# Decays and two delta-rule units in the last HGRN head, and memory pieces in pairs beside the early units

## The reference, cut to what matters

```python
# first layer
h = rmsnorm(x, attn_norm[i]);  mem_n = rmsnorm(mem, mem_norm[i])       # mem: 256 x 1024
cols = split_cols(h @ dsa_w_in[a], DSA_COLS)                           # indexer, latent, queries
k, v = jnp.split(mem_n @ w_kv_mem, 2, axis=-1)                         # memory attention, later
# hybrid layer: 8 HGRN heads, then 8 pairs of delta-rule heads
(hq, hf, hi, hg, gq, gk, gv, ga, gb, gz, gate_h, gate_g) = jnp.split(u @ w_in, offsets, axis=-1)
o_h = rmsnorm_2(hgrn2_chunked(...), hgrn_out_norm) * silu(hg)
qkv = silu(causal_short_conv(concatenate([gq, gk, gv]), conv_w))
beta = sigmoid(gb)
g = -exp(a_log) * softplus(ga + dt_bias)                               # the decays
gam = cumsum(g, axis=-1)                                               # per chunk
```

## Time and profile before

| | |
|---|---|
| median of 3 runs | 3383.93 us (3383.03 to 3387.18) |
| profiled execution | 3391.74 us, its span 3389.9 us |
| TensorE busy | 3216.2 us, 95% |
| VectorE / ScalarE / GpSimd busy | 1580.0 / 1419.1 / 1585.7 us |
| mean granted clock of TensorE | 0.97 of full |
| HBM read | 241.51 MB, 72 GB/s over the span |

### The profile page before, as it was taken

How to read it: one execution, slowest core, us unless ns; L and a number is a source line. 1 busy time by engine, 2 the same in 40 slices (tenths; PEclk the granted TensorE clock), 3 DMA queues, 4 the chain that set the end, 5 groups by cost and what they waited for, 6 DMA issues and landing times.

```text
span 3389.9 us, 44791 instructions
## 1 busy us (share of the span) xinstructions
PE 3216.2 (95%) x16754; PEld 2650.5 (78%) x16754; DVE 1580.0 (47%) x2189; ACT 1419.1 (42%) x2479; POOL 1585.7 (47%) x1361
## 2 busy tenths in 40 slices
PE   5889999999999999999989886999999999999998
PEld 4567888877788887888867775888888888888887
DVE  4783443146533322443077774555565652233321
ACT  3355333226743333333255544544554432243332
POOL 4345444665554456445542222444444434564454
PEclk8989999999999999999999987999999999999999
DMA  4212333341033333333322210111111123333332
GB/s 120 56 38 63 96 96 95 98 126 45 2 93 99 94 97 89 99 93 95 97 64 55 56 44 25 38 38 38 38 38 38 38 56 95 98 93 99 93 94 81
DMA packets 471621, 246.86 MB, mean 73 GB/s; under 512 B 13883, under 2 KB 468774, under 8 KB 471334
## 3 DMA queue, kind: packets, MB, share of 16 engines
q1 hardware_dynamic: 470144, 241.33, 25.2%
q10 hardware_dynamic: 1318, 3.35, 0.3%
HBM read 241.51 MB, written 2.10 MB: 72 GB/s over the span
## 4 chain that ended last, share of the span: by engine, by line
PE 86%; DVE 7%; ACT 3%; issue 3%; POOL 1%; DMA 0%; POOLq 0%; ACTq 0%; DVEq 0%
PE ps L465 19%; PE ps L466 19%; PE ps L467 19%; PE ps L2450 2%; PE ps L2346 2%; PE ps L2347 2%; PE ps L2348 2%; PE ps L2432 2%; PE ps L1645 2%; PE ps L1669 2%; PE ps L1655 2%; PE ps L1865 1%; PE ps L1938 1%; PE ps L1866 1%; PE ps L1867 1%
## 5 line engine op out<-in xcount | busy, mean ns | idle before, releaser
L447 POOL TENSOR_TENSOR w_lo<-ring,w_hi 128x512 fp32r<-128x512 f32 (+1 forms) x908 | 1225.8, 1372 | 1544.7 <-ACT w_hi L438 1544.6
L438 ACT ACTIVATE w_hi<-ring 128x512 fp32r<-128x512 f32 (+1 forms) x908 | 516.6, 618 | 1286.4 <-PE ps L467 1206.7
L465 PE MATMUL ps<-h_hi,w_hi 128*128 128x512 f32 x1776 | 702.0, 395 | 5.1 <-POOL w_lo L447 4.4
L467 PE MATMUL ps<-h_hi,w_lo 128*128 128x512 f32 x1776 | 692.8, 390 | 0.0
L466 PE MATMUL ps<-h_lo,w_hi 128*128 128x512 f32 x1640 | 640.0, 390 | 0.0
L465 PEld LDWEIGHTS ps<-h_hi,w_hi 128*128 128x128 f32 x1776 | 334.4, 188 | 82.2 <-POOL w_lo L447 6.4
L467 PEld LDWEIGHTS ps<-h_hi,w_lo 128*128 128x128 f32 x1776 | 334.3, 188 | 70.1
L466 PEld LDWEIGHTS ps<-h_lo,w_hi 128*128 128x128 f32 x1640 | 308.8, 188 | 68.1 <-issue 4.6
L466 PE MATMUL ps<-a_lo,w_hi 128*128 128x512 f32 x752 | 292.6, 389 | 0.0
L465 PE MATMUL ps<-a_hi,w_hi 128*128 128x512 f32 x720 | 280.8, 390 | 0.0
L467 PE MATMUL ps<-a_hi,w_lo 128*128 128x512 f32 x720 | 280.2, 389 | 0.0
(11 more groups left out here) (463 smaller groups left out, 5670.1 us busy)
## 6 DMA issues: line engine op xcount, KB each, us to landing
ring<-in_ffn_w_in SPq DMA_DIRECT2D x176, 512.0 KB, 3.9
ring<-in_w_in SPq DMA_DIRECT2D x96, 512.0 KB, 4.0
ring<-in_ffn_w_down SPq DMA_DIRECT2D x32, 512.0 KB, 4.1
ring<-in_ffn_w_out SPq DMA_DIRECT2D x32, 512.0 KB, 3.9
ring<-in_w_o SPq DMA_DIRECT2D x16, 512.0 KB, 4.1
ring<-in_w_branch_gdn SPq DMA_DIRECT2D x16, 512.0 KB, 3.7
ring<-in_nsa_w_in SPq DMA_DIRECT2D x15, 512.0 KB, 3.8
ring<-in_dsa_w_in SPq DMA_DIRECT2D x13, 512.0 KB, 4.1
```

The source lines that it names most:

```text
L438: act.activation(w_hi[:, (halves(u) + j) % PIECES, 0:n, :], slot(u)[:, j * n:(j + 1) * n, :], ACT.Copy) \
L447: pool.tensor_tensor(w_lo[:, q % PIECES, 0:n, :], slot(u)[:, j * n:(j + 1) * n, :], w_hi[:, q % PIECES, 0:n, :].bitcast(f32), ALU.subtract ...
L465: pe.matmul(dst, wh, hi(k), start=first and k == 0, stop=False)
L467: ins = pe.matmul(dst, wl, hi(k), start=False, stop=last and k == 2 * n - 1)
```

## The change

First layer: ScalarE takes the memory's root in `act_proj` behind the eviction of unit 0. The pieces are made in pairs, pair n-1 with unit n for n = 1 to 4: on ScalarE behind unit n's eviction, on GpSimd behind its split of unit n+2, on VectorE behind rope n-1. GpSimd clears the tiles behind the last pair.

HGRN's last head: TensorE multiplies unit (0,0) behind levels 1 and 2, half each, and unit (0,1) between state changes and outputs. ScalarE copies AB_BANK behind level 2, rounds unit (0,2) behind level 4 and unit (0,3) behind the head's outputs, and computes the decays' functions between keys and outputs; VectorE does its part of the decays ahead of the last reciprocal; TensorE's transpose follows the last sum. The two small loads and the clearing of `rows` stand at the start of the HGRN stage. The eviction of (0,0) and (0,1) no longer rounds a unit; it waits for `hg_out` = 8 instead of the cleared rows. TensorE's first rows wait for the last root, which frees their banks.

```diff
@@ act_mem_root
-        act.wait_ge(sig("mem_scaled").sem, 1)
@@ dve_mem_norm (act_mem_norm and pool_mem_norm in the same way)
-    def dve_mem_norm(dve, p):
-        dve.wait_ge(sig("mem_scaled").sem, KT)
...
-        for k in range(KT):
+    def dve_mem_norm(dve, p, pair):
+        if pair == 0:
+            dve.wait_ge(sig("mem_scaled").sem, KT)
...
+        for k in (2 * pair, 2 * pair + 1):
             dve_mem_tile(dve, p, k)
@@ act_proj, behind the eviction of unit n
+            if n == 0:
+                act_mem_root(act)
+            elif n <= KT // 2:
+                act_mem_norm(act, p, n - 1)
@@ pool_proj
+        for n, u in enumerate(p["units"]):
             split_unit(pool, u + AHEAD)
+            if 1 <= n <= KT // 2:
+                pool_mem_norm(pool, p, n - 1)
+            if n == KT // 2:
+                pool_zeros(pool, p, norm)
@@ dve_proj, behind rope r
+            if r < KT // 2:
+                dve_mem_norm(dve, p, r)
@@ pe_hgrn
+                elif not more and l == 1:
+                    name, value = hg_evicted(h, HG_Q)
+                    pe.wait_ge(sig(name).sem, value)
+                    pe_gd_quarters(pe, 0, 0, 0, 1)
+                elif not more and l == 2:
+                    pe_gd_quarters(pe, 0, 0, 2, 3)
-        for step in (pe_hgrn_keys, pe_hgrn_changes, pe_hgrn_outputs, pe_hgrn_sum):
-            step(pe, HG_HEADS - 1)
+        pe_hgrn_keys(pe, HG_HEADS - 1)
+        pe_hgrn_changes(pe, HG_HEADS - 1)
+        pe.wait_ge(sig("ab_copied").sem, 1)
+        pe_gd_unit(pe, 0, 1)
+        pe_hgrn_outputs(pe, HG_HEADS - 1)
+        pe_hgrn_sum(pe, HG_HEADS - 1)
+        pe_decays(pe)
@@ act_hgrn
         act.wait_ge(sig("lb_diff").sem, 1)
+        act_load_gdn(act)
...
                     round_unit(act, hg_unit(h + 1, HG_V) if more else gd_units + 1)
+                    if not more:
+                        act_ab_rows(act)
                 elif l == 4:
                     if h:
                         act_hgrn_outputs(act, h - 1)
-                    if more:
-                        round_unit(act, hg_unit(h + 1, HG_G))
+                    round_unit(act, hg_unit(h + 1, HG_G) if more else gd_units + 2)
...
+        act_hgrn_keys(act, HG_HEADS - 1)
+        act_decays(act)
+        act_hgrn_outputs(act, HG_HEADS - 1)
+        round_unit(act, gd_units + 3)
+        act_hgrn_root(act, HG_HEADS - 1)
+        act_columns(act)
@@ dve_hgrn, start and end
+        dve.memset(rows[0:64, :], 0.0).then_inc(sig("rows_clear").sem, 1)
...
         dve_hgrn_states(dve, HG_HEADS - 1)
+        dve_decays(dve, ch)
         dve_hgrn_inverse(dve, ch, HG_HEADS - 1)
@@ new, and the buffers of the decays
+    ab_rows, g_abs = k_end[:, 0, :], k_end[:, 1, :]
+    def act_ab_rows(act):
+        act.wait_ge(unit_done.sem, ab_unit + 1)
+        act.activation(ab_rows[0:64, :], ps[0:64, AB_BANK, :], ACT.Copy).then_inc(sig("ab_copied").sem, 1)
@@ act_load_gdn, pe_gd_rows, pe_gdn, act_gd_evac
-        act.wait_ge(sig("hg_out").sem, HG_HEADS)
+        else:
+            pe.wait_ge(sig("roots").sem, HG_HEADS)
-        pe_decays(pe)
         pe_gd_rows(pe, 0)
-        pe_gd_unit(pe, 0, 0)
-        pe_gd_unit(pe, 0, 1)
         pe_gd_unit(pe, 0, 2)
-                act.wait_ge(sig("rows_clear").sem, 1)
+                act.wait_ge(sig("hg_out").sem, HG_HEADS)
-        round_unit(act, gd_unit(h, j) + AHEAD)
+        if h or j >= 2:
+            round_unit(act, gd_unit(h, j) + AHEAD)
```

More of the change, by code:

```diff
@@ L964, in dve_mem_tile @@
            .then_inc(sig("mem_tile").sem, 1)
[L966 to L972 removed]
+    def dve_mem_norm(dve, p, pair):
+        if pair == 0:
+            dve.wait_ge(sig("mem_scaled").sem, KT)
+            dve.wait_ge(sig("gains_ready").sem, 1)
+            for k in (KT - 2, KT - 1):
+                dve.wait_ge(*tile_ready(plans["attn0"], k))
+        for k in (2 * pair, 2 * pair + 1):
             dve_mem_tile(dve, p, k)
@@ L977, in act_mem_tile, with act_mem_norm @@
         act.activation(n_hi[p["layer"]][:, k, :], mem_tile[:, k % 2, :], ACT.Copy).then_inc(sig("mem_hi").sem, 1)
-    def act_mem_norm(act, p):
-        for k in range(KT):
+    def act_mem_norm(act, p, pair):
+        for k in (2 * pair, 2 * pair + 1):
             act_mem_tile(act, p, k)
@@ L986, in pool_mem_tile, with pool_mem_norm @@
             .then_inc(sig("mem_ready").sem, 1)
-    def pool_mem_norm(pool, p):
-        for k in range(KT):
+    def pool_mem_norm(pool, p, pair):
+        for k in (2 * pair, 2 * pair + 1):
             pool_mem_tile(pool, p, k)
@@ L1108, in pool_zeros, with pool_proj @@
             pool.memset(square_sum[:, 0:128], 0.0).then_inc(sig("pads_zero").sem, 1)
-    def pool_proj(pool, p):
-        for u in p["units"]:
+    def pool_proj(pool, p, norm):
+        for n, u in enumerate(p["units"]):
             split_unit(pool, u + AHEAD)
+            if 1 <= n <= KT // 2:
+                pool_mem_norm(pool, p, n - 1)
+            if n == KT // 2:
+                pool_zeros(pool, p, norm)
     def dve_proj(dve, ch, p, part=-1, first=0, last=99):
@@ L2291, in dve_decays @@
     def dve_decays(dve, ch):
-        dve.wait_ge(sig("hg_out").sem, HG_HEADS)
-        dve.memset(gd_x[:, :, 0:3], 0.0)
-        dve.memset(rows[0:64, :], 0.0).then_inc(sig("rows_clear").sem, 1)
+        g = ab_rows[0:GD_V, :]
         dve.wait_ge(sig("small_loaded").sem, 32)
         dve.wait_ge(sig("gd_scalar").sem, 1)
-        ch.link(dve.tensor_scalar(g_pos[0:GD_V, :], ps[0:GD_V, AB_BANK, :], small[0:GD_V, 0:1], 0.0, ALU.add, ALU.max))
+        ch.link(dve.tensor_scalar(g, g, small[0:GD_V, 0:1], 0.0, ALU.add, ALU.max))
         dve.wait_ge(sig("gd_scalar").sem, 3)
-        ch.link(dve.tensor_tensor(g_pos[0:GD_V, :], g_pos[0:GD_V, :], g_log[0:GD_V, :], ALU.add))
-        ch.link(dve.tensor_scalar(g_pos[0:GD_V, :], g_pos[0:GD_V, :], small[0:GD_V, 2:3], -1.0, ALU.mult, ALU.mult))
+        ch.link(dve.tensor_tensor(g, g, g_abs[0:GD_V, :], ALU.add))
+        ch.link(dve.tensor_scalar(g, g, small[0:GD_V, 2:3], -1.0, ALU.mult, ALU.mult))
         dve.wait_ge(sig("rows_clear").sem, 1)
@@ L2303, in dve_decays, with dve_columns @@
             tok = slice(i * P, (i + 1) * P)
-            ins = dve.tensor_tensor_scan(rows[0:GD_V, tok], ones[0:GD_V, :], g_pos[0:GD_V, tok], 0.0, ALU.mult, ALU.add)
+            ins = dve.tensor_tensor_scan(rows[0:GD_V, tok], ones[0:GD_V, :], g[:, tok], 0.0, ALU.mult, ALU.add)
         ins.then_inc(sig("rows_ready").sem, 1)
+    def dve_columns(dve, ch):
+        dve.wait_ge(sig("hg_out").sem, HG_HEADS)
+        dve.memset(gd_x[:, :, 0:3], 0.0)
         dve.wait_ge(sig("gd_scalar").sem, 5)
@@ L2645, in act_gdn @@
     def act_gdn(act):
-        act_decays(act)
         act_gd_eg(act, 0)
```

28 lines of the change are left out of this document (10 added, 18 removed).

## The result

The median went from 3385.01 us (3383.03 to 3387.18, four runs) to 3348.76 us (3347.69 to 3350.78, four runs): ratio 0.9894, 95% interval 0.988 to 0.9908, a gain of 36.3 us. The forecast was 3346 with a gain of 38.5. The profiled run of the changed kernel took 3348.76 us with a span of 3347.0.

The account below looks back on a forecast made before the run. TensorE, 86% of the chain that ended last, was taken as the bound, with time to win only in its waits and low clock. Gains of 13.5 early and 25 late, 38.5 together, took 3383.9 to 3345.4, stated as 3346; range 3337 to 3361 us.

Parts of the forecast that it names:

- Early: First layer: memory pieces spread beside projection units; TensorE's unit 5 ends at 80.6 instead of 94.0, gain 13.5 us.
- Step 1: Last HGRN head: unit (0,0) in halves behind levels 1 and 2; head 6's square comes 1.0 us earlier.
- Step 2: Last HGRN head: with round_unit behind head 6's square, the step before the reciprocal comes 8.9 us after it, before 6.7.
- Step 3: Last HGRN head: unit (0,1) fills TensorE's 5.9 us wait, running from 2027.4 to 2034.8, near the cold end.
- Step 5: Last HGRN head: the decays, 6.6 us of ScalarE, lie between key copy and outputs at cost 0.
- Step 6: Behind the last head's root: eviction of unit (0,0) from 2049.6 instead of 2068.52, gain 18.9 us.
- Step 7: First two delta-rule convolutions: three taps go from 4.37 to 2.33 us; VectorE gains 4.1, unit (0,2) lets through 3.8.
- Step 8: Delta rule's sums and unit (0,3) no longer start at half clock, as (0,2) runs into them; gain 2.5 us.
- late half falls short: Rival, chance 0.18: units (0,1) and (0,3) at the lower clock, convolutions stay at 4.4; gain 31.5, time 3352 us.
- pieces stall: Rival, chance 0.14: early units exceed the 2 us of cover by about 2 each, 8 in all; time 3353 us.
- Waits stay: Rival, chance 0.02: something else in the last head still ends last, early pieces cost what they save; 3383 us.
- The slower rival: Rival, chance 0.04: TensorE's clock falls in the eight delta-rule heads, +45 us outweighing the gain; time 3390 us.

Follow-up runs that it names:

- decays back: Changed kernel with the decays put back behind the last HGRN head's output, the two units still inside the head; 3360.55 us.
- bank: Changed kernel with unit (0,2) in a bank the last head has left, units (0,2) and (0,3) ahead of the sums, evictions earlier; 3340.4 us.
- quarter first: Changed kernel with one quarter of a projection unit put ahead of the level 4 transposes in each delta-rule head that has a next one; 3337.91 us.
- The quarter: Kernel before, with only a quarter of a projection unit moved ahead of the level 4 transposes in each delta-rule head that has a next one; 3373.85 us.
- late part alone: Kernel before with only the late edits (last HGRN head, decays, first two delta-rule units), memory pieces where they were; 3362.03 us.
- GpSimd beside taps: Changed kernel with four unused GpSimd subtractions added, two beside each of the first two delta-rule convolutions; 3350.61 us.
- pieces in fours: Changed kernel with memory pieces made four per unit beside units 1 and 2 instead of two beside units 1 to 4; 3350.52 us.
- the kernel with the moved roundings: Changed kernel with ScalarE's rounding of unit (0,2) moved behind the decays and that of (0,3) behind the root; 3345.11 us.
- the pair with the quarter: Kernel before and changed kernel, each with a quarter of a projection unit moved ahead of the level 4 transposes; 3373.85 and 3337.91 us.

## Why the prediction was right

The time was right because the large terms were: the early stretch, the decays and the two units under cover. Each step stands beside what the profile shows; times of the late ones count from the square of head 6.

- *Early, 13.5.* Measured 13.47, with a spacing of 6.35, no wait of L1033 and none of L465 for w_lo left. (The recorded ends, 94.0 and 80.6, give 13.4.) That two pieces per unit have cover shows in the absent waits; four lose 2.7, and to GpSimd's w_lo, where the prediction had looked to VectorE and ScalarE.
- *Step 1, square 1.0 earlier.* 1.14 (14.61 in all, less 13.47), and this is luck. The 1.15 were already there at head 5's square (1978.50 before, 1963.88 now), ahead of any edit of the last head; from that square to head 6's it is 39.65 before and 39.66 now. The step itself shows nothing here, and the same stretch with the last head as before took 37.9 in two other profiles, so a gain of 1.0 could not have been told.
- *Step 2, 8.9 to the reciprocal, 2.2 us longer than before.* 8.7, 2.0 longer. The prediction took it as the price of the rounding pair (1.15) by the pattern of the earlier heads. The kernel without it shows the price to be 2.6 and its way: GpSimd's w_lo slows VectorE's step (0.42 to 1.48), TensorE waits 2.91, and its clock falls.
- *Step 3, unit (0,1) in 7.4, near its cold end of 8.2.* Wrong by its size: it took 5.6 (2014.11 to 2019.70), all at full clock. In three other profiles (decays back, bank, quarter first) its first quarter was cold and it took 6.5.
- *Step 4, root's end 24.2.* 23.0, by step 3.
- *Step 5, decays cost 0.* Right: the outputs start as soon as unit (0,1) ends. Put back, they cost 12 us, more than the 6.6 of ScalarE that the prediction counted, for behind the output each hand-over between ScalarE and VectorE stands open as well.
- *Step 6, eviction 32.4 behind, gain 18.9.* 30.9, gain 20.7 with the square's own.
- *Step 7, 3.8 let through.* 4.0 (from one eviction to that of (0,2): 12.57 before, 8.54 now). The wait of 5 to 7 us ahead of unit (0,2) is 4.7.
- *Step 8, 2.5.* 1.6 (from that eviction to the first head: 9.76 before, 8.16 now).

The late sum is 26.3 (1.1 of it the luck of step 1) against 25.2, the place sum 39.8 against 38.7 (38.5 as stated). The measured 36.3 are 2.2 less than the forecast and 3.5 less than the place sum. What differs is TensorE's clock where nothing was edited, which the prediction left out of its sum and put in its range, and it sits first in the kernel before. That kernel's profile lay 6.7 above its median, the changed kernel's on it. The quarter says where those 6.7 may lie: on the kernel before it shortened the profile by 17.9 us, 16.6 of them in the six heads, but the median by 10.2 only. So the median run of the kernel before seems to have had some two long heads fewer than its profile; no trace shows one.

The last HGRN head has two lengths now as well: from square to square 18.5 to 19.3 us in four profiles with that order (changed kernel, late part alone, GpSimd beside taps, pieces in fours), 21.1 or 21.2 in three (decays back, bank, quarter first). In the last of them the granted clock from the square to the outputs was 0.72 (the row below), where the changed kernel had 0.89 and the kernel with the moved roundings 1.00:

```profile
2004.20:2022.70 18.50, 14.91 (x68) 12.29 (x68) 13.92 (x21) 14.76 (x20) 2.67 (x2) 0.72 0.11 29
```

So 2 us of the late gain are given back in part of the runs. The changed kernel's own profile, which lies on its median, has the shorter length, so this doesn't explain the 36.3; in the pair with the quarter, 35.9, it does count, for there the late part shows 23.6 by place instead of 25.1.

Of its signs of being wrong none came: the evictions of (0,0) stand 30.9 behind the square, not over 34, and of the seven steps between openings one changed by more than 2 us (85.3 to 82.0), not each. Its bound of 42.5 for the gain is 1.0 more than its own terms give (13.5 + 28), and its lower bound of 28 has no term of its own; nothing hangs on either.

Of the rivals, *late half falls short* and *pieces stall* named mechanisms that exist (cold units, thin cover) and weren't reached. *Waits stay* fell with the waits. The slower rival, the clock in the heads, was right in its unit, 3.2 us per head, and in its bound; its direction is either way, and it isn't a matter of this change: the kernel before has it, and one quarter of a unit moved takes it away in both kernels, for 10 to 11 us. That is more than the 9.4 by place that went with the two units, and less than the 14.9 that went with the decays.

## What to carry to other kernels

When equal stages of one kernel have two lengths in the same trace, compare them instruction by instruction before tuning anything else: the difference is a cost that comes and goes with unrelated edits, and it makes medians of small edits misleading until it is removed. Judge small edits by the distance between two instructions around the place, not by the total. And count an instruction put on a helper engine by what it sets off: its partner on GpSimd, VectorE's slowdown beside it, and the clock that TensorE loses in the wait.

## What the runs showed of the hardware

- Two stretches equal to 0.01 us, with the same waits before them in their heads, were followed by granted clocks of 1.00 and 0.69; the stretch before the fall does not tell whether it comes. With a wait cut from 2.2 to 0.9 us the later fall was in none of 18 heads and the earlier, 24 us ahead of that wait, in one. Why the earlier one goes is open: the wait is shorter, a quarter has moved, and the heads' period has changed too (82.0 to 81.6), and no run parted these.
- Code that is the same, up to head 5's square, took between 1961.4 and 1966.0 us in nine profiles (the changed kernel and its edits but the pieces in fours): 4.5 us of spread before the edited place. The steps from one HGRN head's square to the next are 38.2 to 39.7 there.
- VectorE instructions with two inputs in SBUF, beside GpSimd: 0.42 to 1.48 (a half tile), 2.33 to 2.99 and 3.65 (three taps) as more of GpSimd's subtractions lies beside them, and 4.37 beside a w_lo pair. The Trainium skill, "SBUF — State Buffer", section "Who interferes with whom", lets such a pair lock each other out for the whole instruction, and these rows agree with it in kind.
